# Turning over the value product of a prompt attention, and rotating its score banks

## The reference, cut to what matters

```python
def block(i):                      # one block of 128 queries
    logits = (jnp.einsum('bqhd,bkhd->bhqk', qb, k).astype(jnp.float32) * scale
              + (fq[..., None] - f_cum[:, :, None, :]))
    logits = jnp.where(qpos[:, None] >= key_pos[None, :], logits, -jnp.inf)
    probs = jax.nn.softmax(logits, axis=-1).astype(v.dtype)
    return jnp.einsum('bhqk,bkhd->bqhd', probs, v)
```

## Time and profile before

| What | us |
|---|---|
| median of three runs | 3488.0 (3482.9 to 3490.4) |
| the profiled execution | 3497.1 |
| its span | 3495.5 |
| prompt attention, within the span | 1789 to 2129 |

### The profile page before, as it was taken

One profiled execution on the slowest core, in us unless ns is written; L12 is line 12 of the kernel. 1 busy time (PEld: TensorE's weight loads), 2 busy tenths in 40 slices (PEclk: granted clock), 3 DMA queues, 4 the chain that ended last, 5 costly groups with the idle time before them and its releaser, 6 DMA issues.

```text
span 3495.5 us, 53221 instructions
## 1 busy us (share of the span) xinstructions
PE 3236.1 (93%) x20292; PEld 3070.4 (88%) x20292; DVE 1632.7 (47%) x2771; ACT 857.1 (25%) x1457; POOL 174.9 (5%) x315
## 2 busy tenths in 40 slices
PE   7999979999999979899979998889799999999878
PEld 6999959999999969799978885449599999999877
DVE  4434373334433374623346774443734333443562
ACT  3111131111111122322245553222321111111221
POOL 1000000000000000000021111220000000000000
PEclk9999989999999989899989999999899999999989
DMA  2111101111111111022132225872011111111111
GB/s 90 43 48 39 47 19 49 43 43 48 45 43 43 49 49 37 25 88 86 52 102 47 57 49 185 295 273 71 18 49 43 43 47 44 42 49 43 56 31 58
DMA packets 221911, 225.88 MB, mean 65 GB/s; under 512 B 9701, under 2 KB 182757, under 8 KB 221746
## 3 DMA queue, kind: packets, MB, share of 16 engines
q1 hardware_dynamic: 196994, 146.82, 13.5%
q0 software_dynamic: 24752, 76.63, 6.9%
HBM read 196.92 MB, written 18.10 MB: 62 GB/s over the span
## 4 chain that ended last, share of the span: by engine, by line
PE 84%; DVE 6%; DMA 3%; ACT 3%; issue 2%; POOL 1%; POOLq 0%; SPq 0%; DVEq 0%; ACTq 0%
PE psum L1539 19%; PE psum L1541 19%; PE psum L1540 19%; PE psum L1554 5%; PE psum L1560 5%; PE psum L1555 5%; PE psum L1844 3%; PE psum L1834 2%; DMA kpage<-in_cache_k 2%; DVE psum L1030 1%; PE psum L1893 1%; DVE y L1036 1%; PE psum L1943 1%; DVE h L1046 1%; PE psum L1822 1%
## 5 line engine op out<-in xcount | busy, mean ns | idle before, releaser
L1539 PE MATMUL psum<-xs_hi,w_hi 128*128 128x384 f32 (+1 forms) x2736 | 893.1, 326 | 9.7 <-DVE y L1245 4.3
L1541 PE MATMUL psum<-xs_hi,w_lo 128*128 128x384 f32 (+1 forms) x2736 | 892.3, 326 | 0.0
L1540 PE MATMUL psum<-xs_lo,w_hi 128*128 128x384 f32 (+1 forms) x2736 | 891.7, 326 | 0.0
L1539 PEld LDWEIGHTS psum<-xs_hi,w_hi 128*128 128x128 f32 x2736 | 513.6, 188 | 11.9 <-DVE y L1245 6.1
L1540 PEld LDWEIGHTS psum<-xs_lo,w_hi 128*128 128x128 f32 x2736 | 513.6, 188 | 0.0
L1541 PEld LDWEIGHTS psum<-xs_hi,w_lo 128*128 128x128 f32 x2736 | 513.6, 188 | 0.0
L1554 PE MATMUL psum<-xs_hi,w_hi 128*128 128x384 f32 (+1 forms) x1104 | 362.8, 333 | 9.5 <-DVE w_lo L1008 3.7
L1555 PE MATMUL psum<-xs_hi,w_lo 128*128 128x384 f32 (+1 forms) x1104 | 360.5, 331 | 0.0
L1541 PE MATMUL psum<-hid_hi,w_lo 128*128 128x384 f32 (+1 forms) x1056 | 346.0, 328 | 0.0
L1540 PE MATMUL psum<-hid_lo,w_hi 128*128 128x384 f32 (+1 forms) x1056 | 345.1, 327 | 0.0
L1539 PE MATMUL psum<-hid_hi,w_hi 128*128 128x384 f32 (+1 forms) x1056 | 344.7, 326 | 0.0
(11 more groups left out here) (257 smaller groups left out, 3883.7 us busy)
## 6 DMA issues: line engine op xcount, KB each, us to landing
kpage<-in_cache_k SPq DMA_DIRECT2D x64, 512.0 KB, 6.0
v_page<-in_cache_v POOLq DMA_DIRECT2D x64, 512.0 KB, 6.3
raw<-in_w_gate SPq DMA_DIRECT2D x44, 512.0 KB, 3.6
raw<-in_w_up SPq DMA_DIRECT2D x44, 512.0 KB, 3.7
raw<-in_w_down SPq DMA_DIRECT2D x44, 512.0 KB, 3.4
raw<-in_w_in SPq DMA_DIRECT2D x24, 512.0 KB, 3.7
raw<-in_w_ple_gate SPq DMA_DIRECT2D x16, 512.0 KB, 3.8
out<-rows_out POOLq DMA_DIRECT2D x16, 512.0 KB, 2.9
```

The costliest lines, as they stand in the source:

```text
L1539: M(out, wh, xh, start=first, stop=False)
L1540: M(out, wh, xl, start=False, stop=False)
L1541: return M(out, wl, xh, start=False, stop=last)
```

## The change

The value product is turned over. The values (128 keys x 64 features) become the stationary operand and the transposed probabilities move through, 128 columns at a time; the result is 64 features x 128 queries, as `qo` needs it, so `o_pair`, `transpose_o` and `take_o` go. Since a result fills 64 partitions, two query blocks go together: the first to partitions 0 to 63 of bank 7 and the second to 64 to 127, in two tiles of 64 columns of the array. The scale is now a number per column. Two further matmuls per pair of items (`rinv`, broadcast to 64 stationary columns, against the identity) write it as rows beside the result, ACT copies those rows to SBUF (`take_rinv`), and DVE multiplies the result by them on its way to `qo` (`normed`, two instructions of 64x128).

The items of a head are now of 8, 7, 2, 1, 6, 5, 4 and 3 key blocks. Their scores rotate through banks 0 to 4 (`S_AT`), and `S_BACK` says how many items back the exponential must be done that frees the banks. There are four `probT` tiles. The hardware loop is gone: all 128 items are written out. The group sizes of the large items are 4+4, 3+4, 2+4 and 1+4, in that order of banks.

```diff
-    probT = [sb(f"probT{i}", [P, 8, P], F32, A_Y + 12928 + 4096 * i) for i in range(2)]
+    probT = [sb(f"probT{i}", [P, 8, P], F32, off) for i, off in
+             enumerate((A_Y, A_Y + 12928, A_Y + 17024, A_Y + 29792))]
     v_keys = sb("v_keys", [P, 8, D], F32, A_XL)
-    o_pair = sb("o_pair", [P, 8, P], F32, A_Y)
     nmx = sb("nmx", [P, 8], F32, A_Y + 4608)
     rsum = sb("rsum", [P, 8], F32, A_Y + 4640)
-    rinv = sb("rinv", [P, 8], F32, A_Y + 4672)
+    rinv = sb("rinv", [P, 4, 1], F32, A_Y + 4672)
+    rinv_row = sb("rinv_row", [P, P], F32, A_Y + 4096)
...
-        ITEMS = [(hh, qb) for hh in range(2) for qb in (7, 0, 6, 1, 5, 2, 4, 3)]
-        NI, HP = len(ITEMS), H // 2
-        OT_AT = 3
+        QBS = (7, 6, 1, 0, 5, 4, 3, 2)
+        NI = len(QBS)
+        NITEMS, NPAIRS = NI * H, NI * H // 2
+        NG, HEADG = [], 0
+        for _qb in QBS:
+            NG.append(HEADG)
+            HEADG += 1 + (_qb > 3)
...
+        S_AT = (0, 2, 4, 0, 1, 3, 0, 2)
+        S_BACK = (2, 2, 5, 3, 3, 3, 3, 3)
+        def s_view(i):
+            nk = (QBS[i % NI] + 1) * P
+            b = S_AT[i % NI]
+            return psum[:, b, 0:nk] if nk <= 512 else psum[:, b:b + 2, :].rearrange("p a b -> p (a b)")[:, 0:nk]
+        def groups(i):
+            nb = QBS[i % NI] + 1
+            g = HEADG * (i // NI) + NG[i % NI]
+            return [(g, 0, nb)] if nb <= 4 else [(g, 0, nb - 4), (g + 1, nb - 4, 4)]
+        def groups_through(i):
+            return groups(i)[-1][0] + 1
+        def o_view(u):
+            return psum[DH * u:DH * u + DH, 7, 0:P]
+        def rinv_view(u):
+            return psum[DH * u:DH * u + DH, 7, P:2 * P]
...
+            def exps(i):
+                act_e.wait_ge(s_max, i + 1)
+                if i >= 2:
+                    act_e.wait_ge(pt_ready, groups_through(i - 2))
+                A(prob[i % 2][:, 0:(QBS[i % NI] + 1) * P], s_view(i), ACT.Exp, bias=nmx[:, i % 4:i % 4 + 1],
+                  accum_out=rsum[:, i % 4:i % 4 + 1]).then_inc(exp_done, 1)
+            def take_probT(i):
+                for g, kb, nb in groups(i):
                     if g % 2 == 0:
-                        act_e.wait_ge(pt_ready, gcount(hp, g + 1))
-                        act_e.wait_ge(pv_done, hp * NI + (j + 1))
-                        A(probT[j % 2][:, kb:kb + nb, :], psum[:, 5, 0:nb * P].rearrange("p (c t) -> p c t", c=nb),
+                        act_e.wait_ge(pt_ready, g + 1)
+                        if i >= 4:
+                            act_e.wait_ge(pv_done, i // 2 - 1)
+                        A(probT[i % 4][:, kb:kb + nb, :], psum[:, 5, 0:nb * P].rearrange("p (c t) -> p c t", c=nb),
                           ACT.Copy).then_inc(pt_act, 1)
-            def take_o(hp, g_ready):
-                act_e.wait_ge(pt_ready, g_ready)
-                A(qo[:, ds(hp, 1), 512:SEQ].rearrange("p o t -> p (o t)"), psum[:, 5, :], ACT.Copy).then_inc(pt_act, 1)
-            def pair(hp, first, last):
-                for j in range(NI):
-                    if not (last and j == NI - 1):
-                        exps(hp, j + 1)
-                    take_probT(hp, j)
-                    if j == 2:
-                        split(hp, 1)
-                    elif j == 10 and not last:
-                        split(hp + 1, 0)
-                    if j == 1 and not first:
-                        take_o(hp - 1, gcount(hp, OT_AT + 2))
-            split(0, 0)
-            exps(0, 0)
-            pair(0, True, False)
-            with act_e.Fori(1, HP - 1) as hp:
-                pair(hp, False, False)
-            pair(HP - 1, False, True)
-            take_o(HP - 1, 26 * HP)
+            def take_rinv(p):
+                act_e.wait_ge(pv_done, p + 1)
+                if p:
+                    act_e.wait_ge(o_taken, p)
+                A(rinv_row[:, :], psum[:, 7, P:2 * P], ACT.Copy).then_inc(rinv_row_ready, 1)
+            split(0)
+            exps(0)
+            for i in range(NITEMS):
+                if i + 1 < NITEMS:
+                    exps(i + 1)
+                take_probT(i)
+                if i % 2 and i > 1:
+                    take_rinv(i // 2 - 1)
+                if i % NI == 2 and i // NI + 1 < H:
+                    split(i // NI + 1)
+            take_rinv(NPAIRS - 1)
...
-            def normed(hp, j):
-                it = hp * NI
-                hh, qb = ITEMS[j]
-                dve.wait_ge(exp_done, it + (j + 5))
-                V.reciprocal(rinv[:, j % 2:j % 2 + 1], rsum[:, j % 4:j % 4 + 1]).then_inc(rinv_s, 1)
-                dve.wait_ge(rinv_s, it + (j + 1))
-                dve.wait_ge(pv_done, it + (j + 3))
-                V.tensor_scalar(o_pair[:, qb, DH * hh:DH * hh + DH], psum[:, 7, 0:DH], rinv[:, j % 2:j % 2 + 1],
-                                None, ALU.mult).then_inc(o_taken, 1)
...
+            def inverse(p):
+                dve.wait_ge(exp_done, 2 * p + 2)
+                c = 2 * (p % 2)
+                V.reciprocal(rinv[:, c:c + 2, 0], rsum[:, c:c + 2]).then_inc(rinv_s, 1)
+            def normed(p):
+                dve.wait_ge(rinv_row_ready, p + 1)
+                head = 2 * p // NI
+                r0 = DH * (head % 2)
+                for u in range(2):
+                    qb = QBS[(2 * p + u) % NI]
+                    ins = V.tensor_tensor(qo[r0:r0 + DH, head // 2, qb * P:qb * P + P], o_view(u),
+                                          rinv_row[DH * u:DH * u + DH, :], ALU.mult)
+                ins.then_inc(o_taken, 1)
+            split(0)
+            maxes(0)
+            maxes(1)
+            for i in range(NITEMS):
+                if i + 2 < NITEMS:
+                    maxes(i + 2)
+                take_probT(i)
+                if i % 2 and i > 1:
+                    normed(i // 2 - 1)
+                if i % NI == 3 and i // NI + 1 < H:
+                    split(i // NI + 1)
+                if i % 2:
+                    inverse(i // 2)
+            normed(NPAIRS - 1)
...
+            def scores(i):
+                g, qb = i // NI, QBS[i % NI]
+                hh, b = g % 2, S_AT[i % NI]
+                if i % NI == 0:
+                    pe.wait_ge(aug_landed[hh], 32 * (g // 2 + 1))
+                    pe.wait_ge(split_act, 3 * g + 3)
+                    pe.wait_ge(split_dve, 2 * g + 2)
+                if i >= S_BACK[i % NI]:
+                    pe.wait_ge(exp_done, i - S_BACK[i % NI] + 1)
...
-            def outputs(hp, j):
-                hh, qb = ITEMS[j]
-                for g, kb, nb in groups(j):
-                    pe.wait_ge((pt_act, pt_dve)[g % 2], ghalf(hp, g - g % 2) + 2)
-                pe.wait_ge(o_taken, hp * NI + (j + 1))
-                for c in range(qb + 1):
-                    ins = M(psum[:, 7, 0:DH], probT[j % 2][:, c, :],
-                            v_keys[:, c, ds(hp * P + DH * hh, DH)], start=c == 0, stop=c == qb)
+            def outputs(p):
+                head = 2 * p // NI
+                if p >= 1:
+                    pe.wait_ge(o_taken, p)
+                through = groups_through(2 * p + 1)
+                pe.wait_ge(pt_act, (through + 1) // 2)
+                pe.wait_ge(pt_dve, through // 2)
+                nb = [QBS[(2 * p + u) % NI] + 1 for u in range(2)]
+                for c in range(nb[0]):
+                    for u in range(2):
+                        if c < nb[u]:
+                            M(o_view(u), v_keys[:, c, DH * head:DH * head + DH], probT[(2 * p + u) % 4][:, c, :],
+                              start=c == 0, stop=c == nb[u] - 1)
+                pe.wait_ge(rinv_s, p + 1)
+                for u in range(2):
+                    ins = M(rinv_view(u), rinv[:, 2 * (p % 2) + u, :].broadcast_to([P, DH]), ident[:, :],
+                            start=True, stop=True)
                 ins.then_inc(pv_done, 1)
-            def transpose_o(hp, dve0, act0):
-                pe.wait_ge(o_taken, hp * NI + (NI + 1))
-                for r in range(2):
-                    pe.wait_ge((pt_dve, pt_act)[r], (dve0, act0)[r] + 1)
-                    for c in range(4):
-                        ins = nc.tensor.transpose(psum[:, 6 - r, c * P:(c + 1) * P], o_pair[:, 4 * r + c, :], ident[:, :])
-                    ins.then_inc(pt_ready, 1)```

How the instructions now stand. On PE, in the fifth turn of a head: first before the change, two turns of the loop with items of 7 and 2 key blocks (`L1834` transposes, `L1844` is the value product, `L1822` to `L1825` are scores).

```order
L1834 MATMUL psum<-ident,prob_127 128x128 x7
L1844 MATMUL psum<-v_keys,probT_130 128x64
L1822 MATMUL psum<-k_hh_116,q_hl_120 128x384
L1823 MATMUL psum<-k_low_118,q_high_122 128x384
L1825 MATMUL psum<-causal_r,ident_r 128x128
L1834 MATMUL psum<-ident,prob_128 128x128 x2
L1844 MATMUL psum<-v_keys,probT_129 128x64 x7
```

(84 more changed lines are left out.)

86 lines of the change are left out of this document (22 added, 64 removed).

## The result

The changed kernel is slower: its median is 3510.7 us (8 runs, 3506.9 to 3515.2), against 3491.1 for the kernel before (8 runs, 3482.9 to 3498.5). The ratio is 1.0054, with a 95% interval of 1.0043 to 1.0065, or 19.6 us. The forecast was no change, 3487.

The account below looks back on a forecast made before the run. PE was taken to bound the prompt attention, with DVE and ACT feeding it in strict order. Terms -6 (heads), -1.5 (half-clock start) and +6.6 (clock falls) sum to -1: 3488 - 1 = 3487 us, range 3458 to 3514.

Parts of the forecast that it names:

- The chain and its gap: Second pair's scale matmuls wait on an 8.0 us chain through ACT and DVE; PE stands still about 2.2 us a head.
- Tiles side by side: Value product: two 64-column tiles run together, 40 x 0.109 = 4.4 us a head against 8.0; rival, not side by side: 3515, chance 0.06.
- A head without falls of the clock: Steady prompt attention: 8.0 + 11.6 = 19.6 us a head, 0.4 less than before; -6 us over 14 heads.
- The clock: Steady prompt attention, behind the new gap: 3 falls in 14 heads at 2.2 us each, +6.6 us.
- all 14: 3511: Extreme of the rival on falling clock: a fall behind the scale matmuls' wait in all 14 heads, 3511 us.
- most heads: Rival: clock falls behind the wait on `rinv_s` in most heads, 2.2 us a fall, 3496 at 7 falls; chance 0.20.
- the neighbourhood in the earlier trace is emptier: Argument against frequent falls: the next stage, where a 1.80 us wait preceded a low clock, has less work around it.
- The start: First heads: the first two gain nothing, ending where the third's data lands; the half-clock stretch behind gains 1.5 us.
- The end: After the last head: next stage's keys load when the last outputs are done, as before; no term in the sum.

Follow-up runs that it names:

- experiment 6: Changed kernel with all value passes of a pair's first query block ahead of its second's, instead of alternating; 3539.4 us in one run, 23.06 us a head.
- experiment 1: Changed kernel with 36 dummy passes on PE ahead of the second pair's wait for reciprocals, no wait removed; 3496.3 us, ratio 1.001.
- experiment 7: Splits spread over a head's turns, reciprocals ahead of them: first kernel, on the changed kernel, 3469.7 us; second, also with old item order and banks, 3464.5 us.
- experiment 2: Changed kernel with the reciprocals ahead of DVE's two splits instead of behind them; 3496.5 us, ratio 1.0014.
- experiment 4: Kernel before with one added PE wait for DVE's first split ahead of one value product in every head but the last; 3558.0 us in one run.
- experiment 5: Changed kernel with 16 dummy passes on PE ahead of the second pair's wait for reciprocals; 3480.6 us in one run, beside 3493.3 for the kernel before.
- experiment 8: Kernel before with only the splits spread over a head's turns, from the second pair of heads on; 3550.5 us, ratio 1.0171.

## Why the prediction went wrong, step by step

- **The chain and its gap: right.** 8.0 us through ACT and DVE and 2.2 us of idle PE were forecast ahead of the `rinv` matmuls of the second pair. In the trace the chain shown above takes 8.25 (from PE's start at 1998.81 to 2007.06), and PE's idle time is 2.05 and 1.96, two heads in turn, in every head.
- **Tiles side by side: right** as to the term, 40 x 0.109; experiment 6 shows what the other case is, and that it hangs on the order in the program.
- **A head without falls of the clock:** forecast 19.6, measured 19.88 with the gap filled (experiment 1). The sum of chain and work was near; 0.3 x 14 = 4 us of the gain were not there. PE's own work was put too low: 15.8 us a head, against the 16.6 of busy PE in the first kernel of experiment 7, where no fall of the clock lengthens it.
- **The clock: this step failed.** The sum took "3 falls in 14 heads at 2.2 us: +6.6". The clock fell in every steady head. The price of a fall was put slightly too high (2.2, measured 1.74), and the last head has no splits behind it and so no gap, so the term should have been 13 x 1.74 = +23. With it the sum, -6 - 1.5 + 23, is +15 (rounded), beside +18 between the two traces; that the two come so close is partly luck, as the next two points and the 0.3 above show. I had written down this case, "all 14: 3511", and gave "most heads" 0.20. What I set against it, that the neighbourhood in the earlier trace rows is emptier, was the error: PE was busy for 94% of the 6 us ahead of the gap and the clock fell all the same. The remark that some waits of 1.8 us in that stage don't lower the clock took the weight off the one row that showed a fall, and no row showed a wait of 2 us at a busy place that was harmless. (Experiments 2, 4 and 6 show some of 1.8 to 2.3 us that were; in the changed kernel itself none was.)
- **The start:** a gain of 1.5 was forecast for the half-clock stretch; up to the fifth head's split it was 5. From the third head's split to the fourth's are 21.9 us instead of 28.2, and the stretch at half clock was shorter (0.80 over the second ten us, against 0.50 in the earlier trace rows); the head behind it, with its gap and fall, gives 1.4 back.
- **The end:** 2.6 us lost between the last head's split and the first page. The clock of 0.95 there, 1.00 before, is the thirteenth fall, from 2116.6 to 2120.0, behind the gap that the last splits make; at 1.74 us it is the larger part of the 2.6. The rest the sum left out: two long waits follow one another with little work between (1.27 and 1.17 us ahead of L1830 and L1873), as the last pairs have no next head's scores beside them. This division is an estimate, since the first page also waits for its data. Another 3.4 us went in the stage behind, which no edit touches. That stage took from 1356 to 1370 us in the twelve traces of this study, without an order that I can see, so I count it as scatter between executions; this is not shown.

The stretches of the last point, after and before, all engines as above:

```profile
2107.90:2147.60 39.70, 30.12 (x283) 24.41 (x283) 23.70 (x54) 18.31 (x46) 0.00 (x0) 0.95 0.07 18
2095.80:2132.90 37.10, 31.19 (x242) 27.83 (x240) 23.04 (x60) 17.58 (x39) 0.00 (x0) 1.00 0.06 18
```

The Trainium skill's page TensorE: Matmul & The Clock Gate (HAM oscillation) warns of waits between bursts of matmuls that put the array back to the half clock each time. In the changed kernel the trace agrees: one fall a head, at 1.74 us each. The waits of the page's own example last some 3 to 5 us; here 2.0 were enough, and in experiments 2 and 6 waits of 2.29 and 2.05 us were harmless in some heads, so the page alone would not have told this case.

## What to carry to other kernels

Where a chain through two feeding engines leaves the matrix engine idle for 2 us once in 20, price the clock's fall in every turn, not in some: it came 13 times in 13 here, and 8, 12 and 10 times in 13 or 14 in experiments 2, 4 and 6. Here it turned a gain of 0.2 us a head into a loss of 1.56. Before rearranging the matmuls, look at what stands behind the longest block of work on the feeding engines (here DVE's splits): by the medians spreading it was worth 41 us on the changed kernel, against the 14 that filling the gap gave back, because it takes both the gap and the fall. Let column tiles alternate in the program: in turn they didn't share the array (experiment 6).

## What the runs showed of the hardware

- A wait's length doesn't decide alone. 1.96 to 2.05 us lowered the clock in 13 of 13 heads of the changed kernel, but 1.95 to 2.05 in 10 of 13 of experiment 6; 2.19 to 2.29 did in 8 of 13 of experiment 2; 1.81 did in 12 of 14 of experiment 4; 1.1 to 1.2 did in none of experiment 5, and 1.11, once or twice a head, in 10 of 13 of experiment 8.
- How long the clock stays low differs too: 3.4 to 6.8 us in the changed kernel, and with the old value product up to 23.9 (experiment 4) and 20.5 (experiment 8, with PE fully busy). No run tells why.
- Two 64-column tiles finish two fp32 passes of 128 columns per 0.109 us if the program alternates between them, and one per 0.109 us if it doesn't.
- The scaling from PSUM by a row, 64x128, takes 286 ns on DVE, beside 0.28 for the 128x64 one by a number per partition.
